# A transformer block in float32: the latent attention's queries and keys turned on VectorE and through DRAM

## The chip, the cores and the metric

The kernel runs on one core of one Trainium2 chip. The metric is the device time of one execution in microseconds (us), lower is better. Of three executions of the kernel before, the median is 890.19 us (889.85 to 890.6).

## The reference, cut to what matters

The program computes a long transformer block for 256 rows of 1024 columns in float32: a gated feed-forward, a mixer of three branches, a second gated feed-forward, and then a second block (a modulated short convolution and a third feed-forward). The mixer holds two attentions. The first is over memory rows. The second is the latent attention with 8 heads, causal, and it is the one that is changed:

```
q = (rmsnorm(c_q, cq_norm) @ w_uq).reshape(B, S, 8, 96)      # S = 256 rows
q = rmsnorm(q, q_norm);  q = concat([q[..., :64], rope(q[..., 64:])])
kv = (rmsnorm(c_kv, ckv_norm) @ w_ukv).reshape(B, S, 8, 128)
k = rmsnorm(concat([k_nope, k_pe]), k_norm);  k = concat([k[..., :64], rope(k[..., 64:])])
s = einsum('bqhd,bkhd->bhqk', q, k) * 96 ** -0.5             # masked, softmax, times v
```

TensorE's matmul sums over partitions. The scores of a head therefore need q and k with the 96 columns of the head on the partitions, while the products leave them with the rows on the partitions: each head's queries and keys must be turned.

The second block is modulated by six rows, `silu(c) @ ada_w + ada_b`, each of 1024 values. The kernel calls c the conditioning.

## The kernel before

**Weights.** All weights stream through one ring of 10 slots in SBUF (`RAW`, tile raw). An entry is a *unit*: two chunks of 128 rows of one product's weights, 128x1024 values, 512 KB. SP's queue fetches entry n+10 once entry n is used up (L1765). ScalarE copies a unit to a rounded high part (`split`, L916), VectorE subtracts it to get the low part (`split`, L1209), and TensorE multiplies high by high, high by low and low by high (L741 to L743), which for one unit and both halves of the rows is 12 matmuls with 512 columns. There are 308 units.

**Order.** `schedule()` writes one list, SCHEDULE, and every engine's queue is the part of that list that it has a function for. `unit(name, i, *steps)` first adds the `split` steps up to four units ahead (AHEAD), then the matmuls, then the side steps. So VectorE and ScalarE have the copies for unit u + 4 in their queues ahead of the side steps of unit u. In the mixer the side steps are given by a table `side`, from the mixer's unit number, 0 to 67, to steps. An engine that waits in one step holds all of its later ones. SP's queue, too, is one list: a fetch stands behind every wait ahead of it.

**Modulation rows.** `stream_of()` mixes 48 further entries of 512 KB into the ring, ("ada", i), each 128 columns of `ada_w`. They are not multiplied on TensorE: VectorE multiplies each by the conditioning row and sums it (L1221). 24 of them run in the first feed-forward (66 units), 24 in the second. The first goes behind unit 10 of the feed-forward, and after that they go at 24 in 50 units:

```
            while ada and i >= 10 and (24 - len(ada)) * 50 < (i - 9) * 24:
                out.append(ada.pop(0))
```

Also in the first feed-forward: at unit 8 SP fetches the memory rows in two forms, 2 MB in all; and the hidden rows are turned without TensorE, in six groups: VectorE turns 32x32 blocks (`blocks`, L1337), SP writes the result to DRAM in four pieces (`spill`, L1820), reads it back in another order (`reload`, L1827), and ScalarE and VectorE make high and low parts of it (`inner`, L998 and L1342). The first group is written at unit 11, reloaded at unit 12 and used by ScalarE at unit 14.

**The latent attention.** Products uq0, uq1, ukv0, ukv1 fill QT and KT, 128 partitions x 2 x 768. `row1` (sums of squares), `row2` (the keys times their norm) and `row3` (rotary part, for q half 0 at unit 30, q half 1 at 32, k half 0 at 33, k half 1 at 34) finish them on VectorE. Then each head goes through five steps that are spread over units by `att`:

```
    def att(k):
        parts = (("att_val", k - 4), ("att_pt", k - 3), ("att_sc", k - 1), ("att_in", k), ("att_exp", k - 1))
        return [p for p in parts if 0 <= p[1] < 8]
    for n in range(12):
        side[37 + 2 * n] = side.get(37 + 2 * n, []) + att(n)
```

`att_in(h)` turns a head: four TensorE transposes into PSUM (L850), then two ScalarE copies with the norm's gain into qkT (L1123, L1124). `att_sc` multiplies scores (L858), VectorE masks them and takes maxima (L1544 to L1549), ScalarE exponentiates (`att_exp`, L1133), TensorE turns the weights (`att_pt`, L865) and multiplies them with V (`att_val`, L874), and VectorE scales the result into U (L1563). TensorE's small results share four PSUM banks in turn (`bank`).

**Around it.** Branch a, the spatial gating: VectorE normalizes V (`sv_norm`, L1485 and L1488; half 0 at unit 32, half 1 at unit 35), TensorE mixes it (`su` at unit 38, L840), VectorE forms two products (L1494, L1500), and TensorE turns the result (`y_turn` "a" at unit 41, L649). Gate additions (L1572, each behind its product's last unit) share VectorE. Branch b, the attention's result, is turned at unit 61 (`y_turn` "b", L649, L1097, L1467), and its product's units are 66 and 67. The conditioning row is loaded for the second time at unit 41, into acc2.

## Time and profile before

| | before |
|---|---|
| median of three executions | 890.19 us |
| the profiled execution | 890.65 us |
| its span, first to last instruction | 888.9 us |
| TensorE (PE) busy | 878.5 us, 99% |
| VectorE (DVE) busy | 631.6 us, 71% |
| ScalarE (ACT) busy | 460.7 us, 52% |
| granted TensorE clock, mean | 0.997 |

The profiled execution took 890.65 us, its span is 888.9 us; the rest lies around the span. Starts of matmuls are recorded, while their ends are modelled, so a busy engine is best read from the distance between starts. A time in the lists is counted from the start of the span. PEld is TensorE's loading of the stationary operand, which overlaps with the matmuls. Lines are those of the kernel before. Where the text counts units, it counts from the start of a feed-forward or, in the mixer, from the mixer's first unit.

### The profile page before, as it was taken

To read this page: it belongs to the slowest core of one execution; us is meant where nothing else is said; L and a number is where in the kernel's file an instruction comes from. 1 tells how busy PE (TensorE), PEld (TensorE's weight loads), DVE (VectorE), ACT (ScalarE), POOL (GpSimd) and SP (SyncE) were. 2 spreads that over 40 slices of the span, in tenths; PEclk is the share of its full clock that TensorE was granted. 3 is DMA by queue.
4 is the path that set the end of the run, shared out by engine and by line. 5 is a ranking of instruction groups with operands and counts; after the bars stand their busy time and mean duration, and the time that the engine had idled before them with its cause. 6 is when DMAs were issued, how large, how long until landed. Compare 5 with 4: busy or idle time off the path is not lost.

```text
span 888.9 us, 11084 instructions
## 1 busy us (share of the span) xinstructions
PE 878.5 (99%) x4079; PEld 732.8 (82%) x4079; DVE 631.6 (71%) x883; ACT 460.7 (52%) x697; POOL 40.8 (5%) x66
## 2 busy tenths in 40 slices
PE   9999999999999999999999999999999999999996
PEld 7878888888998888888888888888888888888885
DVE  6769987837558877688578886875768766665743
ACT  6546554626688475446535554454445344444530
POOL 0010000022103000000000000001000100000000
PEclk9999999999999999999999999999999999999998
DMA  9899999774654454454699999975755577777741
GB/s 365 346 323 352 359 363 351 270 237 145 182 175 175 162 193 164 149 186 143 218 308 348 344 329 323 333 257 163 257 179 177 182 248 241 240 233 246 250 120 47
DMA packets 94879, 215.12 MB, mean 242 GB/s; under 512 B 14520, under 2 KB 46185, under 8 KB 94697
## 3 DMA queue, kind: packets, MB, share of 16 engines
q1 hardware_dynamic: 94104, 212.97, 69.8%
q10 hardware_dynamic: 720, 1.44, 0.4%
q8 instruction: 32, 0.52, 0.2%
q14 instruction: 23, 0.18, 0.1%
HBM read 204.66 MB, written 9.72 MB: 241 GB/s over the span
## 4 chain that ended last, share of the span: by engine, by line
PE 94%; DMA 2%; DVE 1%; issue 1%; ACT 1%; SPq 0%; POOL 0%; POOLq 0%; DVEq 0%
PE ps L741 29%; PE ps L743 29%; PE ps L742 29%; DMA t_raw<-in_f_up 2%; PE ps L679 1%; PE ps L656 1%; PE ps L649 1%; PE ps L858 1%; PE ps L874 1%; PE ps L816 0%; PE ps L850 0%; PE ps L798 0%; DVE t_wl L1209 0%; DMA t_acc<-in_xT 0%; PE ps L865 0%
## 5 line engine op out<-in xcount | busy, mean ns | idle before, releaser
L1209 DVE TENSOR_TENSOR t_wl<-t_raw,t_wh 128x1024 fp32r<-128x1024 f32 (+3 forms) x308 | 360.4, 1203 | 103.3 <-ACT t_wh L916 102.4
L916 ACT ACTIVATE t_wh<-t_raw 128x1024 fp32r<-128x1024 f32 (+3 forms) x308 | 307.8, 1040 | 106.9 <-DMA t_raw<-in_f_up 63.3
L741 PE MATMUL ps<-t_wh,t_XH 128*128 128x512 f32 (+2 forms) x640 | 250.2, 391 | 1.3 <-DVE t_wl L1209 1.3
L743 PE MATMUL ps<-t_wh,t_XL 128*128 128x512 f32 (+2 forms) x640 | 247.1, 386 | 0.0
L742 PE MATMUL ps<-t_wl,t_XH 128*128 128x512 f32 (+2 forms) x640 | 246.8, 386 | 0.0
L741 PEld LDWEIGHTS ps<-t_wh,t_XH 128*128 128x128 f32 x640 | 120.2, 188 | 24.8 <-DVE t_wl L1209 2.1
L743 PEld LDWEIGHTS ps<-t_wh,t_XL 128*128 128x128 f32 x640 | 120.1, 188 | 24.0
L742 PEld LDWEIGHTS ps<-t_wl,t_XH 128*128 128x128 f32 x640 | 120.3, 188 | 22.9
L741 PE MATMUL ps<-t_wh,t_YH 128*128 128x512 f32 x288 | 113.1, 393 | 0.2 <-DVE t_YL L1634 0.2
L743 PE MATMUL ps<-t_wh,t_YL 128*128 128x512 f32 x288 | 112.2, 390 | 0.0
L742 PE MATMUL ps<-t_wl,t_YH 128*128 128x512 f32 x288 | 112.2, 389 | 0.0
L741 PE MATMUL ps<-t_wh,t_HH 128*128 128x512 f32 x264 | 103.0, 390 | 0.0
L743 PE MATMUL ps<-t_wh,t_HL 128*128 128x512 f32 x264 | 102.8, 389 | 0.0
L742 PE MATMUL ps<-t_wl,t_HH 128*128 128x512 f32 x264 | 102.7, 389 | 0.0
L741 PEld LDWEIGHTS ps<-t_wh,t_YH 128*128 128x128 f32 x288 | 54.1, 188 | 11.5 <-issue 0.6
L743 PEld LDWEIGHTS ps<-t_wh,t_YL 128*128 128x128 f32 x288 | 54.1, 188 | 11.2
L742 PEld LDWEIGHTS ps<-t_wl,t_YH 128*128 128x128 f32 x288 | 54.1, 188 | 10.9
L1221 DVE CUSTOM_DVE_ANT_0 t_acc<-t_raw,t_acc 128x1024 f32<-128x1024 f32 x48 | 58.3, 1214 | 6.5 <-issue 3.9
L741 PEld LDWEIGHTS ps<-t_wh,t_HH 128*128 128x128 f32 x264 | 49.6, 188 | 10.4
L743 PEld LDWEIGHTS ps<-t_wh,t_HL 128*128 128x128 f32 x264 | 49.6, 188 | 10.3
L742 PEld LDWEIGHTS ps<-t_wl,t_HH 128*128 128x128 f32 x264 | 49.6, 188 | 10.2
L998 ACT ACTIVATE t_HH<-t_tp 128x512 fp32r<-128x512 f32 (+1 forms) x36 | 19.4, 587 | 40.5 <-DMA t_tp<-inner_rows 40.5
(225 smaller groups left out, 614.1 us busy)
## 6 DMA issues: line engine op xcount, KB each, us to landing
t_raw<-in_f_up SPq DMA_DIRECT2D x130, 512.0 KB, 5.6
t_raw<-in_f_dn SPq DMA_DIRECT2D x66, 512.0 KB, 5.5
t_raw<-in_ada SPq DMA_DIRECT2D x48, 512.0 KB, 6.3
inner_rows<-t_tp SPq DMA_DIRECT2D x60, 128.0 KB, 3.8
t_tp<-inner_rows SPq DMA_DIRECT2D x15, 512.0 KB, 5.2
t_raw<-in_mkv SPq DMA_DIRECT2D x8, 512.0 KB, 3.6
t_raw<-in_ga SPq DMA_DIRECT2D x8, 512.0 KB, 3.3
t_raw<-in_gc SPq DMA_DIRECT2D x8, 512.0 KB, 3.2
```

The source lines that it names most:

```text
L649: m = pe.transpose(o, src[:, t, (c + i) * P:(c + i) * P + P], ident[:, :])
L656: m = pe.transpose(ps[:, b, c * P:c * P + P], src[:, t, (4 * j + c) * P:(4 * j + c) * P + P], ident[:, :])
L679: x = pe.matmul(ps[:, bank_of("f1_up0", t), :], a[:, k, t * P:t * P + P], w, start=a is XH and not last and k == 0, stop=last and k == KC - 1)
L741: pe.matmul(o, xh, h, start=k == 0, stop=False)
L742: pe.matmul(o, xh, l, start=False, stop=False)
L743: x = pe.matmul(o, xl, h, start=False, stop=k == n - 1)
L858: m = pe.matmul(ps[:, b, t * P:t * P + n], qkT[0:96, t * P:t * P + P], qkT[0:96, 256:256 + n], start=True, stop=True)
L874: m = pe.matmul(ps[:, b, t * 64:t * 64 + 64], pT[:, j * P:j * P + P], VT[:, kt, h * 64:h * 64 + 64], start=kt == 0, stop=kt == t)
L916: act.activation(wh[:, m % SPL, lo:w], raw[:, n % RAW, lo:w], ACT.Copy).then_inc(hi_made, 1)
L998: act.activation(parts_of(HH, q, t), placed(q, t), ACT.Copy).then_inc(*hid_hi.by(f, q, t))
L1209: dve.tensor_tensor(wl[:, n % RAW, lo:w], raw[:, n % RAW, lo:w], wh[:, m % SPL, lo:w].bitcast(F32), ALU.subtract).then_inc(drained, 1)
L1221: dve.tensor_tensor_reduce(out=acc2[:, 1, :], in0=r, in1=cond, scale=1.0, scalar=0.0, op0=ALU.mult, op1=ALU.add, accum_out=mod[:, i:i + 1] ...
```

## The change

Four things are changed.

1. `att_in` has no part on TensorE any more. VectorE turns 32x32 blocks of all heads' queries (`qk_blocks` "q" at mixer unit 33) and keys (at unit 35), two instructions of 128x768 for each. SP writes them to DRAM in four pieces each (`qk_out`, units 34 and 36) and reads them back with the head's columns on 96 partitions (`qk_back`, units 35 and 37). ScalarE's two copies into qkT now read SBUF; the first head's wait for both reloads.
2. The attention's steps start at unit 39 instead of 37, and branch b is turned at unit 63 instead of 61.
3. The 24 modulation rows of the first feed-forward start behind unit 18 instead of 10 and go at 24 in 42 units.
4. The queries come back into acc2, where the conditioning row went; this is loaded at unit 57 instead of 41, behind the eighth head's copies. The keys come back into a new tile KB, which lies over QT and a part of KT.

```diff
+        start = 18 if tag == "f1" else 10
         for i, u in enumerate(part):
             out.append(u)
-            while ada and i >= 10 and (24 - len(ada)) * 50 < (i - 9) * 24:
+            while ada and i >= start and (24 - len(ada)) * (60 - start) < (i - start + 1) * 24:
                 out.append(ada.pop(0))
...
-            35: [("sv_norm", 1)], 38: [("su", 0), ("su", 1)], 41: [("y_turn", "a", 0), ("y_turn", "a", 1), ("load_cond", 1)],
-            61: [("y_turn", "b", 0), ("y_turn", "b", 1)]}
+            35: [("sv_norm", 1)], 38: [("su", 0), ("su", 1)], 41: [("y_turn", "a", 0), ("y_turn", "a", 1)],
+            57: [("load_cond", 1)], 63: [("y_turn", "b", 0), ("y_turn", "b", 1)]}
...
+    for n, x, step in ((33, "q", "qk_blocks"), (34, "q", "qk_out"), (35, "q", "qk_back"),
+                       (35, "k", "qk_blocks"), (36, "k", "qk_out"), (37, "k", "qk_back")):
+        side[n] = side.get(n, []) + [(step, x)]
     for n in range(12):
-        side[37 + 2 * n] = side.get(37 + 2 * n, []) + att(n)
+        side[39 + 2 * n] = side.get(39 + 2 * n, []) + att(n)
...
+        qk_mid = {"q": hn[:, :, :].rearrange("p t d -> p (t d)")[:, 0:1536], "k": QT[:, :, :].rearrange("p t d -> p (t d)")}
+        qk_end = {"q": acc2[:, :, :].rearrange("p t d -> p (t d)"), "k": KB[:, :]}
...
-            def att_in(h):
-                b = bank(("att_in", h), qkt_made, h + 1)
-                if h == 0:
-                    pe.wait_ge(*qk_made.at("k", 1))
-                for i, src in enumerate((QT, KT)):
-                    for t in (0, 1):
-                        m = pe.transpose(ps[0:96, b, i * 256 + t * P:i * 256 + t * P + P], src[:, t, h * 96:h * 96 + 96], ident[:, :])
-                m.then_inc(turned, 1)
...
             def att_in(h):
-                b, full = place["att_in", h]
-                act.wait_ge(turned, full)
                 if h:
                     act.wait_ge(turned, place["att_sc", h - 1][1])
-                act.activation(qkT[0:96, 0:256], ps[0:96, b, 0:256], ACT.Copy, scale=qkg[0:96, 0:1])
-                act.activation(qkT[0:96, 256:512], ps[0:96, b, 256:512], ACT.Copy, scale=qkg[0:96, 1:2]).then_inc(qkt_made, 1)
+                else:
+                    act.wait_ge(qk_in["q"], 16)
+                    act.wait_ge(qk_in["k"], 16)
+                for n, x in enumerate("qk"):
+                    m = act.activation(qkT[0:96, 256 * n:256 * n + 256].rearrange("p (t i n) -> p t i n", t=2, i=4),
+                                       qk_end[x][0:96].rearrange("p (i t h n) -> p h t i n", i=4, t=2, h=8)[:, h],
+                                       ACT.Copy, scale=qkg[0:96, n:n + 1])
+                m.then_inc(qkt_made, 1)
...
+            def qk_blocks(x):
+                dve.wait_ge(*qk_made.at(x, 1))
+                for t in (0, 1):
+                    m = dve.transpose(qk_mid[x][:, 768 * t:768 * t + 768].rearrange("p (j h n) -> p h j n", j=3, h=8),
+                                      (QT if x == "q" else KT)[:, t, :].rearrange("p (h j n) -> p h j n", j=3, h=8))
+                m.then_inc(qk_blocked[x], 1)
...
             def load_cond(n):
                 if n:
-                    sp.wait_ge(*qk_mean.at("k", 1))
+                    sp.wait_ge(qkt_made, 8)
...
+            def qk_out(x):
+                sp.wait_ge(qk_blocked[x], 1)
+                for i in range(4):
+                    sp.dma_start(qk_rows["qk".index(x), i].rearrange("b f e -> f b e"),
+                                 qk_mid[x][32 * i:32 * i + 32, :].rearrange("f (b e) -> f b e", b=6)).then_inc(qk_out_done[x], 16)
+            def qk_back(x):
+                sp.wait_ge(qk_out_done[x], 64)
+                sp.dma_start(qk_end[x][0:96].rearrange("p (b e) -> p b e", b=8),
+                             qk_rows["qk".index(x)].rearrange("i (t j) f e -> (j f) (i t) e", t=2)).then_inc(qk_in[x], 16)
```

## Rows read from the trace of the kernel before

**Rows 1.** The page: busy time by engine, share of span, instructions.
```profile
PE 878.5 (99%) x4079; PEld 732.8 (82%) x4079; DVE 631.6 (71%) x883; ACT 460.7 (52%) x697; POOL 40.8 (5%) x66
```

**Rows 2.** TensorE's timeline: start, duration, line, operation; idle before and releaser.
```profile
57.55 0.39 PE L743 MATMUL ps<-t_wh,t_XL 128*128 128x512 f32 x1
59.08 0.50 PE L741 MATMUL ps<-t_wh,t_XH 128*128 128x512 f32 x1 [1.15 <-DVE t_wl L1209]
...
61.71 0.39 PE L743 MATMUL ps<-t_wh,t_XL 128*128 128x512 f32 x1
62.25 0.50 PE L741 MATMUL ps<-t_wh,t_XH 128*128 128x512 f32 x1 [0.16 <-DVE t_wl L1209]
```

**Rows 3.** Chain of waits, 25 to 70 us: start, duration, what.
```profile
50.32 6.36 DMA t_raw<-in_f_up
```

**Rows 4.** ScalarE's timeline, 45 to 60 us.
```profile
53.80 1.15 ACT L998 ACTIVATE t_HH<-t_tp 128x512 fp32r<-128x512 f32 x2 [4.43 <-DMA t_tp<-inner_rows]
...
56.70 1.06 ACT L916 ACTIVATE t_wh<-t_raw 128x1024 fp32r<-128x1024 f32 x1 [0.72 <-DMA t_raw<-in_f_up]
```

**Rows 5.** Two stretches: length, busy time by engine, clock, DMA share, GB/s.
```profile
62.00:110.00 48.00, 47.84 (x211) 39.53 (x211) 46.89 (x84) 28.40 (x45) 0.00 (x0) 1.00 0.97 347
290.00:310.00 20.00, 19.98 (x107) 16.80 (x106) 16.07 (x26) 7.97 (x14) 0.00 (x0) 1.00 0.46 158
```

**Rows 6.** Chain of waits, 293.5 to 304 us.
```profile
294.23 0.61 PE ps L850 x4
...
302.78 0.44 PE ps L850 x4
```

**Rows 7.** TensorE's timeline around the turning of the second head.
```profile
301.96 0.82 PE L858 MATMUL ps<-t_qkT 96*128 96x128 f32 x4
...
303.29 0.39 PE L742 MATMUL ps<-t_wl,t_XH 128*128 128x512 f32 x1
```

**Rows 8.** TensorE's timeline around the last scores.
```profile
353.89 0.82 PE L858 MATMUL ps<-t_qkT 96*128 96x128 f32 x4
...
354.78 0.40 PE L742 MATMUL ps<-t_wl,t_XH 128*128 128x512 f32 x1
```

**Rows 9.** Line 1337: duration in ns, minimum, median, maximum; forms.
```profile
L1337 DVE STREAM_TRANSPOSE t_tp<-t_hp x18: 711/1245/1248, 34.4 to 826.3; 128x1024 f32<-128x1024 f32 x15, 128x512 f32<-128x512 f32 x3
```

**Rows 10.** VectorE's timeline, 289 to 306 us.
```profile
290.61 1.22 DVE L1209 TENSOR_TENSOR t_wl<-t_raw,t_wh 128x1024 fp32r<-128x1024 f32 x1
...
295.92 0.69 DVE L1488 TENSOR_TENSOR t_V<-t_V,t_gates 128x512 f32<-128x512 f32 x1
...
298.80 1.28 DVE L1572 TENSOR_TENSOR t_gates<-ps,t_bgate 128x512 f32<-128x512 f32 x2
...
304.91 0.69 DVE L1500 TENSOR_TENSOR t_U<-t_U,t_V 128x512 f32<-128x512 f32 x1
```

**Rows 11.** TensorE's timeline around the spatial matmuls.
```profile
297.44 1.95 PE L840 MATMUL ps<-t_V,t_sgw 128*128 128x128 f32 x16
299.14 0.48 PE L741 MATMUL ps<-t_wh,t_XH 128*128 128x512 f32 x1
```

**Rows 12.** Timeline of all engines and SP's queue, 122 to 131 us.
```profile
122.33 2.01 SPq L1820 DMA_DIRECT2D inner_rows<-t_tp  x4
...
126.30 0.38 SPq L1827 DMA_DIRECT2D t_tp<-inner_rows  x1
...
130.75 0.63 ACT L998 ACTIVATE t_HH<-t_tp 128x512 fp32r<-128x512 f32 x1 [4.92 <-DMA t_tp<-inner_rows]
```

**Rows 13.** Timeline of all engines, 379 to 382 us.
```profile
379.04 1.03 PE L649 MATMUL ps<-t_ident,t_U 128*128 128x128 f32 x8
...
380.30 1.29 DVE L1467 TENSOR_TENSOR t_YL<-ps,t_YH 128x512 fp32r<-128x512 f32 x2 [3.87 <-ACT t_YH L1097]
```

**Rows 14.** Timeline of all engines, 147 to 149.5 us.
```profile
147.14 1.23 DVE L1209 TENSOR_TENSOR t_wl<-t_raw,t_wh 128x1024 fp32r<-128x1024 f32 x1 [4.24 <-ACT t_wh L916]
...
149.45 0.39 PE L741 MATMUL ps<-t_wh,t_HH 128*128 128x512 f32 x1
```

More of the change, by code:

```diff
@@ L423, in build @@
             MV = sb("MV", [P, 2, 512], F32, c)
-            QT = sb("QT", [P, 2, 768], F32, c)
-            KT = sb("KT", [P, 2, 768], F32, c)
+            with ExitStack() as c2:
+                QT = sb("QT", [P, 2, 768], F32, c2)
+                KT = sb("KT", [P, 2, 768], F32, c2)
+            KB = sb("KB", [P, 2048], F32, c)
+            sb("qk_rest", [P, 1024], F32, c)
             VT = sb("VT", [P, 2, 512], F32, c)
@@ L484, in build @@
         drop = nc.dram_tensor("mod_rows", (48, P), F32, kind="Internal").ap()
+        qk_rows = nc.dram_tensor("qk_rows", (2, 4, 6, 32, 256), F32, kind="Internal").ap()
         inner_rows = nc.dram_tensor("inner_rows", (4, 8, 32, P), F32, kind="Internal").ap()
@@ L551, in build @@
         k_rope = sem("k_rope")
+        qk_blocked, qk_out_done, qk_in = ({x: sem(f"qk_{n}_{x}") for x in "qk"} for n in ("blocked", "out", "in"))
         v_cent, v_sq, v_mean, v_rstd, v_made = (sem("v_" + n) for n in ("cent", "sq", "mean", "rstd", "made"))
@@ L899, in _ @@
                     "mem_in": mem_in_, "mem_sc": mem_sc, "mem_pt": mem_pt, "mem_val": mem_val, "y_turn": y_turn,
-                    "su": su, "att_in": att_in, "att_sc": att_sc, "att_pt": att_pt, "att_val": att_val,
+                    "su": su, "att_sc": att_sc, "att_pt": att_pt, "att_val": att_val,
                     "mturn": mturn, "conv_turn": conv_turn, "gate_turn": gate_turn}
@@ L1654, in _ @@
                     "sv_mean": sv_mean, "sv_sq": sv_sq, "sv_norm": sv_norm, "su": su, "row1": row1, "row2": row2, "row3": row3,
-                    "att_sc": att_sc, "att_pt": att_pt, "att_val": att_val, "gate": gate, "merge": merge,
+                    "qk_blocks": qk_blocks, "att_sc": att_sc, "att_pt": att_pt, "att_val": att_val, "gate": gate, "merge": merge,
                     "mturn": mturn, "conv_uu": conv_uu, "conv_taps": conv_taps, "gate_turn": gate_turn, "gate_low": gate_low,
@@ L1872, in _ @@
                     "load_cond": load_cond, "ada_rows": ada_rows, "load_mod": load_mod,
-                    "load_mid": load_mid, "gate": gate, "load_final": load_final, "final": final, "spill": spill, "reload": reload}
+                    "load_mid": load_mid, "gate": gate, "load_final": load_final, "final": final, "spill": spill, "reload": reload, "qk_out": qk_out, "qk_back": qk_back}
             for name, *args in SCHEDULE:
```

## The prediction

> **What bounds the kernel now.** I read the page first: TensorE is busy for 878.5 us, 99% of the span [rows 1]. In such a kernel only two things shorten the run: matmul instructions taken off TensorE, and waits of TensorE. So the next view is TensorE's own timeline, looking for starts further apart than usual. The twelve matmuls of one weight unit start at 59.08 (first) to 61.71 (last): 0.1 us extra behind the first, then 0.23 each, 2.72 us a unit. Between the entry and the attention there are two wide gaps: 57.55 to 59.08 and 61.71 to 62.25, both ended by VectorE's low part of a weight unit; less the usual 0.23 they cost 1.3 and 0.3 us, 1.6 in all [rows 2]. The chain of waits says what lies under it: a weight transfer asked for at 50.3 us that landed 6.4 us later [rows 3]. ScalarE's timeline says what stood in its queue ahead of the unit concerned, number 19: the high part of the reloaded hidden rows (start 53.80), a square of the memory rows, and then the unit's own copy at 56.70, which waited 0.72 us for the transfer; ScalarE was free from 56.0 [rows 4]. From there to 110 us the DMA engines are 97% busy and VectorE 46.9 of 48 us [rows 5]: this stretch is near two other limits. In the attention TensorE's timeline has no such gap; there the price of an edit is what TensorE itself executes, plus any wait that is made new.
>
> **Part 1: the turning leaves TensorE.** Removed are 8 heads of 4 transposes. In the chain one head's four take 0.44 us, and the first head's takes 0.61 since they came behind a wait [rows 6]. The timeline agrees: with them [rows 7], from the first score matmul to the second weight matmul it is 301.96 to 303.29 = 1.33 us; after the last head, where none follow, 353.89 to 354.78 = 0.89 [rows 8]. So 7 x 0.44 + 0.6 = **3.7 us off TensorE**. Nothing hides this term, as TensorE is the bound.
>
> The Trainium skill speaks against this edit: VectorE: DVE Perf Modes, section "Rules for kernel authors", gives a 128x128 transpose to TensorE when PSUM may be its destination, as VectorE turns only 32x32 blocks. By that rule the path without TensorE would cost more than 3.7 us; by the rows so far it costs less, and rival C is the case in which the rule has it.
>
> **Part 2: what comes in on VectorE.** Four block transposes of 128x768. The trace has 128x1024 at 1.24 and 128x512 at 0.71 us [rows 9], hence 0.98 each alone, and some 0.1 less back to back, as its neighbours overlap: 1.8 us per pair (1.6 to 2.4, if the scattered output costs as much as a 128x1024 one). The queries' pair goes in right behind the first rotary step of the keys, before the subtraction at 290.61; VectorE has no gap from there to 299. So everything after is 1.8 us later on VectorE, up to the second V normalization, whose addition starts at 295.92 and ends at 296.61 [rows 10]. That one matters: TensorE's spatial matmuls wait for it and now start at 297.44 [rows 11], 0.83 us after it. New: it ends at 298.4, while TensorE arrives at 296.8, as the first head's 0.6 us ahead of it is gone. **A new wait of 1.6 us.** (The low part for the unit between, 1.1 us long, is ready at 293.6 and wanted at about 294.0, so it just holds.)
>
> The keys' pair goes in behind that addition. VectorE: 298.4 + 1.8 = 300.2, then two weight subtractions (2.3), so the gate additions start at 302.5 in place of 298.80. From their start to the end of the second product for branch a it is now 304.91 + 0.69 - 298.80 = 6.8 us [rows 10], new end 309.3. TensorE: spatial matmuls 298.45 to 300.15 (1.70 as now, [rows 11]), three units of 12 matmuls (2.72 each and 0.1 for the first), so it reaches the turning of branch a at 308.4, the second half at 308.85, and waits for the second product until 309.35: **0.5 us**. It is done with it at 309.8 and wants the first scores.
>
> **Part 3: the way through DRAM.** The keys' route ends last. The nearest row is the hidden rows' route of the same form: blocks ended at 122.3, the four writes issued from 122.33, the reload issued at 126.30, ScalarE's first use at 130.75: 8.4 us [rows 12]. Here each way has 786 KB in place of 512, but 1 KB pieces in place of 512 B and DMA engines that are 46% busy from 290 to 310 us rather than 97% [rows 5]. I take 9 us: 300.2 + 9.0 = 309.2, and ScalarE's two copies (0.9) give 310.1 against TensorE's 309.8: **0.3 us**. Bounds: 7.5 us for the route would hide it (slack 1.2); 13 us (each of the two ways 2.3 us longer than its row) costs 4.3. Queued behind this wait: on ScalarE, which blocks at it from about 306, the copies of mixer units 44 and 45, wanted by TensorE only at about 317 and 320 (scores 0.7 us, two units, scores), while their copies and subtractions can be done 3 to 5 us behind the first head's: at least 3 us of cover more than the scores have; on SP's queue, which blocks first for the queries' blocks (about 286 to 292), then for each write, the fetches of four weight units, each some 6 to 9 us late, with ten slots in the ring and about 18 us until they are wanted. Both are hidden as long as the first scores are the ones that wait.
>
> **Other edits of the middle.** The step order of the heads is kept, two matmul units later each; ScalarE's copies read the same 256 elements from SBUF, and their PSUM banks now turn over between three users. Later by two units is the turning of branch b. Its low part comes 1.3 + 1.3 us after TensorE's start (379.04, end 381.6, [rows 13]); it now has two units, 5.4 us, instead of four before the product that wants it. Late next would be the first product of branch b, from a delay of about 2.5 us. The conditioning row, fetched 16 units later, is wanted more than ten units after that. All three: nothing.
>
> **Part 4: the modulation rows of the first feed-forward.** The 24 of them start after unit 18 instead of 10 and are denser (one in 1.75 units instead of 2.08). The ring holds ten entries, and an entry is a weight unit or such a row. Without the rows, ten entries are ten units: unit 19 is asked for when unit 10 is done (unit 11 starts eight units ahead of 57.8, the undelayed start of unit 19: 57.8 - 8 x 2.72 = 36 us) and not behind the reload at 50.3, so its landing no longer counts. ScalarE's queue still has the reload in front: if that lands as now, unit 19's copy starts at 56.0 rather than 56.70 and 0.7 us are gained; if two fewer 512 KB transfers ahead of the write bring it 1 to 2 us sooner, the wait is gone, and the small one at 62.25 with it. Bounds 0.7 and 1.6; I take **1.2 us gained**. From unit 24 to 60 the look-ahead is six units where it was six or seven, and the entries per unit grow from 1.48 to 1.57, or 6%, in a stretch that is 97% busy. A narrow place late in it is unit 52: low part ended 148.4, wanted 149.45 [rows 14], 1.1 us of cover. I cost this at nothing, as the rows' total up to there is the same to within one; without the cover each 1 us is 1 us.
>
> **Sum.** -3.7 + 1.6 + 0.5 + 0.3 - 1.2 = -2.5. The profiled execution took 890.65 us (span 888.9 and 1.8 around it), 0.46 above the median of 890.19. So 888.15 for it, and **887.7 as median**.
>
> **Rivals.** For orientation: +-0.2% is 1.8 us, about what a measurement of this kernel can tell from no change.
> A. The waits are covered: VectorE's pairs cost less at their place, the route takes under 8 us, and the early wait goes whole. -3.7 - 1.6 = -5.3, median 884.9. Against it: VectorE has no gap before 298.8, so at least 1.4 of the 1.6 should show. Partly so (one wait smaller) is inside the forecast's own range.
> B. The early wait stays, because it hangs on the 2 MB of memory rows and on the reload in ScalarE's queue and not on the modulation rows: -3.7 + 2.4 = -1.3, median 888.9, no change that can be told. For it: the reload alone holds unit 19 until 56.0.
> C. Slower: the route through DRAM. ScalarE stops at the first head until the keys are back, and TensorE at its scores. Each microsecond beyond 9 is one lost; it decides (above +1.8) from 13.3 us for the route. With 14.5 us: -2.5 + 5.5 = +3.0, median 893.2. For it: two transfers in a row that each carry half as much again, and a queue that issues them one behind the other. Against it: 8.4 us for the smaller route with the DMA engines twice as busy.
> D. The denser modulation rows empty the ring towards unit 52 and again at 85 to 110 us, where VectorE is nearly full: one or two waits of 1 to 2 us, together 2.5: median 890.2, the same.
>
> **How the numbers follow.** Forecast 0.45, A 0.15, B 0.20, C 0.11, D 0.09. The forecast's own range is 886.6 (route hidden, early gain 1.6, pairs of 1.6 us) to 889.7 (route 10.5 us, early gain 0.7). For 8 in 10 over all cases: from A's 884.9 to 891.0, which holds B and D and leaves out most of C and D's bad end. Faster by over 0.2% (below 888.4): three quarters of the forecast (0.34), A, and a quarter of B (0.05): 0.54. Slower (above 892.0): C's greater part and a little of D: 0.11. The same: 0.35.
>
> **What would show it.** No PE wait at 57 to 62 us, or a smaller one (part 4). Four block transposes of about 0.9 us near 290.6 and 298.4. PE waiting about 1.6 us at the spatial matmuls for V, and 0.5 at branch a's turning for U. The reload of the keys at about 304 and its landing at 308 to 309; ScalarE's qkT copy ended by that landing. Wrong would be the forecast if VectorE had slack ahead of V, if PE waited over 3 us at the first scores, or if PE waits showed up between 70 and 160 us.

## The result and the profile after

The changed kernel takes 902.44 us (median of 4 executions, 902.02 to 904.82) against 890.33 us for the kernel before (4 executions). The ratio is 1.0142 with a 95% interval of 1.0124 to 1.016: slower by some 12 us, where 2.5 us faster was predicted. Its profiled execution took 902.61 us, span 900.9.

The page answers to [rows 1] in busy time by engine. Each engine does what it did, TensorE 32 instructions less; the 12 us are waits.

```profile
PE 878.8 (98%) x4047; PEld 729.9 (81%) x4047; DVE 634.7 (70%) x887; ACT 459.9 (51%) x697; POOL 43.2 (5%) x66
```

TensorE's waits by line and releaser: us in total, times, longest.

```profile
PE ps L865 <- ACT t_qkT L1132: 5.6, 1, 5.6
PE ps L757 <- DVE t_wl L1220: 5.0, 6, 1.8
...
PE ps L856 <- issue: 1.5, 1, 1.5
PE ps L695 <- ACT t_wh L958: 0.8, 2, 0.6
```

L757 is the weight matmul (L741 before), L865 the scores, L856 the spatial matmuls. L695 belongs to the first product; its waits lie before 17 us, where the two kernels are still 0.05 us apart. I then subtracted the starts of the same weight unit's matmuls in the two traces. This offset is -0.44 us at unit 20 of the first feed-forward (62 us), 1.64 at unit 33, 2.93 at unit 40, 5.78 at unit 48 (145 us), and stays there until the attention. It falls to 5.2 (the first head's transposes are gone), rises to 6.9 at the spatial matmuls and to 13.4 behind the first scores, falls by 0.44 per further head to 10.3, and ends at 11.9, as the heads' last steps, two units later than before, are then made up. So there are two losses of about 6 us each, 150 us apart.

**The first feed-forward.** The stretch of [rows 5], columns as there. TensorE's busy time is 1.3 us short of the 48, but it started 201 matmuls instead of 211, and the offset grew by 2.7 us from 62 to 110 us. The DMA engines were busy less (0.86 instead of 0.97) and VectorE too (44.33 us instead of 46.89): none of the three was busy throughout.

```profile
62.00:110.00 48.00, 46.69 (x201) 37.10 (x201) 44.33 (x80) 23.68 (x36) 0.00 (x0) 1.00 0.86 314
```

The chain from 40 to 62 us begins at SP's issue of the hidden rows' writes (L1839), goes through their landing and the reload's, and comes to VectorE's blocks of the next group (L1348), which are what SP waits for again:

```profile
43.26 5.84 DMA inner_rows<-t_tp
49.12 3.89 DMA t_tp<-inner_rows
...
58.25 1.26 DVE t_tp L1348
59.53 0.33 SPq L1839
```

In the timeline of the same stretch the reload had landed at 53.0, 0.8 us sooner than before. ScalarE stood 10.72 us for it (4.43 before, [rows 4]) because it had made the copies ahead of it sooner, not because it came late. VectorE multiplied two modulation rows (L1232) before the low part at 60.54:

```profile
53.03 1.16 ACT L1005 ACTIVATE t_HH<-t_tp 128x512 fp32r<-128x512 f32 x2 [10.72 <-DMA t_tp<-inner_rows]
...
54.91 1.22 DVE L1232 CUSTOM_DVE_ANT_0 t_acc<-t_raw,t_acc 128x1024 f32<-128x1024 f32 x1
...
59.42 1.18 DVE L1232 CUSTOM_DVE_ANT_0 t_acc<-t_raw,t_acc 128x1024 f32<-128x1024 f32 x1
...
60.54 1.22 DVE L1220 TENSOR_TENSOR t_wl<-t_raw,t_wh 128x1024 fp32r<-128x1024 f32 x1
```

The low part at 60.54 is what TensorE waited 1.3 us for at unit 20. It stood behind the blocks (58.25) and the row at 59.42 on VectorE; in the kernel before, one row ran at 55.67 and the next only at 62.12, behind that low part. The wait at unit 19 [rows 2] is gone.

**The attention.** The timeline of all engines around the way of the keys:

```profile
296.45 1.83 DVE L1552 STREAM_TRANSPOSE t_hn<-t_QT 128x768 f32<-128x768 f32 x2
...
302.35 0.39 PE L759 MATMUL ps<-t_wh,t_XL 128*128 128x512 f32 x1
...
303.14 0.30 SPq L1856 DMA_DIRECT2D t_acc<-qk_rows  x1
303.49 0.69 DVE L1499 TENSOR_TENSOR t_V<-t_V,t_gates 128x512 f32<-128x512 f32 x1
...
304.10 1.83 DVE L1552 STREAM_TRANSPOSE t_QT<-t_KT 128x768 f32<-128x768 f32 x2
...
304.28 2.02 PE L856 MATMUL ps<-t_V,t_sgw 128*128 128x128 f32 x16 [1.54 <-issue]
...
305.95 3.03 SPq L1851 DMA_DIRECT2D qk_rows<-t_QT  x4
...
314.48 0.30 SPq L1856 DMA_DIRECT2D t_KB<-qk_rows  x1
...
320.19 0.51 ACT L1132 ACTIVATE t_qkT<-t_acc,t_sc 96x256 f32<-96x256 f32 x1 [8.26 <-DMA t_KB<-qk_rows]
```

Both pairs of blocks took 1.83 us. TensorE's spatial matmuls came 1.93 us after the matmul ahead of them, 1.70 more than the usual 0.23. The keys' route took from 305.9 (blocks ended) to 320.19: 14.3 us, of which 8.5 passed until all four writes had landed and the reload could be issued, and 5.7 for the reload. TensorE's timeline of the first scores and of what follows:

```profile
321.24 1.20 PE L865 MATMUL ps<-t_qkT 96*128 96x128 f32 x3 [5.57 <-ACT t_qkT L1132]
...
322.31 0.99 PE L757 MATMUL ps<-t_wh,t_XH 128*128 128x512 f32 x1
323.09 0.63 PE L758 MATMUL ps<-t_wl,t_XH 128*128 128x512 f32 x1
323.52 0.63 PE L759 MATMUL ps<-t_wh,t_XL 128*128 128x512 f32 x1
...
325.23 0.48 PE L757 MATMUL ps<-t_wh,t_XH 128*128 128x512 f32 x1
325.54 0.40 PE L758 MATMUL ps<-t_wl,t_XH 128*128 128x512 f32 x1
```

Behind the wait of 5.6 us the weight matmuls start 0.43 us apart instead of 0.23, until 325.2. The windows give a granted clock of 0.83 from 310 to 330 us, where the stretches around have 1.00: for some 4 us TensorE ran at the lower of its two levels, 1.2 GHz. From the first score matmul to the second weight matmul it is 1.85 us where it was 0.89 [rows 8], and from there to 325.54 it is 2.45 where six distances of 0.227 make 1.36. The slower starts cost 2.05 us on top of the wait.

```profile
310.00:330.00 20.00, 14.33 (x61) 11.59 (x59) 10.96 (x16) 10.78 (x20) 0.00 (x0) 0.83 0.66 226
```

### The profile page after: what moved, and what is told of

Same layout as the page of the kernel before. It is cut to its first block, busy times and chain, and to the rows that moved or that the text cites. A ratio compares the mean times of both kernels' runs of the same rounds, so it can differ in the third digit from the quotient of the medians.

```text
span 900.9 us, 11027 instructions
## 1 busy us (share of the span) xinstructions
PE 878.8 (98%) x4047; PEld 729.9 (81%) x4047; DVE 634.7 (70%) x887; ACT 459.9 (51%) x697; POOL 43.2 (5%) x66
## 4 chain that ended last, share of the span: by engine, by line
PE 79%; DVE 8%; DMA 7%; ACT 2%; issue 2%; SPq 1%; POOL 0%; POOLq 0%; ACTq 0%; DVEq 0%
PE ps L757 25%; PE ps L759 25%; PE ps L758 25%; DVE t_wl L1220 3%; DMA t_raw<-in_f_up 2%; DMA inner_rows<-t_tp 1%; DMA t_tp<-inner_rows 1%; PE ps L672 1%; PE ps L695 1%; DVE t_acc L1232 1%; SPq L1839 1%; ACT t_wh L923 1%; PE ps L865 1%; DMA qk_rows<-t_QT 1%; DMA t_hn<-in_xT 1%
## 5 line engine op out<-in xcount | busy, mean ns | idle before, releaser
L757 PE MATMUL ps<-t_wh,t_XH 128*128 128x512 f32 (+2 forms) x640 | 251.8, 393 | 3.3 <-DVE t_wl L1220 3.2
L757 PEld LDWEIGHTS ps<-t_wh,t_XH 128*128 128x128 f32 x640 | 120.6, 188 | 29.3 <-DVE t_wl L1220 6.5
L757 PE MATMUL ps<-t_wh,t_YH 128*128 128x512 f32 x288 | 113.4, 394 | 0.2 <-DVE t_YL L1653 0.2
L757 PE MATMUL ps<-t_wh,t_HH 128*128 128x512 f32 x264 | 103.1, 391 | 1.8 <-DVE t_wl L1220 1.8
L757 PEld LDWEIGHTS ps<-t_wh,t_YH 128*128 128x128 f32 x288 | 54.1, 188 | 11.6 <-issue 0.6
L758 PEld LDWEIGHTS ps<-t_wl,t_YH 128*128 128x128 f32 x288 | 54.1, 188 | 10.9
L757 PEld LDWEIGHTS ps<-t_wh,t_HH 128*128 128x128 f32 x264 | 49.6, 188 | 12.6 <-DVE t_wl L1220 2.2
L1232 DVE CUSTOM_DVE_ANT_0 t_acc<-t_raw,t_acc 128x1024 f32<-128x1024 f32 x48 | 58.3, 1214 | 0.0
L1353 DVE TENSOR_TENSOR t_HL<-t_tp,t_HH 128x512 fp32r<-128x512 f32 (+1 forms) x36 | 21.6, 643 | 29.6 <-ACT t_HH L1005 29.6
```

The lines of the kernel that those rows point to most:

```text
L757: pe.matmul(o, xh, h, start=k == 0, stop=False)
L758: pe.matmul(o, xh, l, start=False, stop=False)
L1232: dve.tensor_tensor_reduce(out=acc2[:, 1, :], in0=r, in1=cond, scale=1.0, scalar=0.0, op0=ALU.mult, op1=ALU.add, accum_out=mod[:, i:i + 1] ...
L1353: dve.tensor_tensor(parts_of(HL, q, t), placed(q, t), parts_of(HH, q, t).bitcast(F32), ALU.subtract).then_inc(*hid_lo.by(f, q, t))
```

## The experiments

Each ratio is to the kernel before, run on the same chip. "Alone" means the kernel before with that one edit.

### Which part costs what

The modulation rows alone (`r1_rows18`, its edit is shown), and the changed kernel with the old rows (`r2_way10`, which sets `start = 10` in the changed kernel).

```diff
-            while ada and i >= 10 and (24 - len(ada)) * 50 < (i - 9) * 24:
+            start, end = (18, 60) if tag == "f1" else (10, 60)
+            while ada and i >= start and (24 - len(ada)) * (end - start) < (i - start + 1) * 24:
```

> The kernel before with part 3 of the change alone (modulation rows of the first feed-forward behind unit 18 instead of 10, 24 in 42 units). If the two halves of the change add up, this one gives the 5.8 us by which the mixer starts later in the changed kernel: about 896. Rival: the way through DRAM's queue steps and the rows interact (both load SP's queue), then this alone is under 893.

> The changed kernel with the modulation rows back at unit 10, 24 in 50 units. If the halves add up: 902.4 - 5.8 = about 896.5, with the 5.6 us wait at the first scores as in the changed kernel. Rival: in the changed kernel the wait was long because of what the first feed-forward had displaced; then it is under 3 us here and the time under 893.

Measured: rows alone 896.95 us, 1.0063 (1.0041 to 1.0084); the route with the old rows 896.5 us, 1.0062 (1.004 to 1.0084). The two add up to 1.0125, the whole is 1.0142 (1.0124 to 1.016): within the intervals they are the whole. In the first, TensorE's waits for low parts are 5.1 us in 6, as in the changed kernel; in the second, 6.1 us at the first scores and 1.5 for V. Each half of the change is slower by itself, and for its own reason. In the profiled execution of `r1_rows18` 1.7 us of the loss is the clock: behind a wait of 1.81 us at unit 48 the weight matmuls start 0.43 us apart from 144.8 to 147.8, and the granted clock from 110 to 160 us is 0.97. The changed kernel had a wait of 1.76 us at the same unit and kept a clock of 1.00.

### The rows: later, or denser

The same line with (10, 52), 24 rows in 42 units but from unit 10, and with (18, 65), from unit 18 but in 47 units.

> The kernel before with the rows as dense as in the change (24 in 42 units) but from unit 10 on, so they end at unit 52. Theory look-ahead: ten ring entries are only six units wherever rows are dense, and the loop of VectorE's blocks, SP's waits, fetch and ScalarE's copy cannot be run through in six units; so this loses 4 to 6 us as well, about 895. Rival position: what hurts is that the rows' products are moved into units 24 to 60, behind the memory rows' parts and the rotary tables on VectorE; then this is within 1.5 us of before.

> The kernel before with the rows behind unit 18 but nearly as sparse as before (24 in 47 units, one in 1.96), up to unit 65. Theory look-ahead: part of the units keep seven units of look-ahead, so the loss falls well below that of the dense order: 0 to 2.5 us, 890 to 892.5. Rival position: the loss stays at 4 us or more.

Measured: from unit 10 and dense 898.65 us, 1.0078 (1.0051 to 1.0106); from unit 18 and less dense 891.69 us, 1.0004 (0.9993 to 1.0015). (In the first, 1.7 us more of TensorE's waits are for the turning of the rows themselves.) So the later start by itself shows no cost and no gain; the density costs the 5 to 6 us, although it is a change from one row in 1.96 units (47) to one in 1.75 (42).

### What a row loads

With the rows of `r1_rows18`: each of the 24 rows fetched at half its bytes (`m1_half_bytes`; the multiplication reads the half twice), or fetched whole and multiplied in half its columns (`m2_half_vector`). The modulation that comes out is not the reference's in either. And the kernel before with `RAW = 9`, one slot less in the ring (`m6_ring9`). Of the first edit the line with the width is shown.

```diff
-    return 1024 if name == "ada" else W_OF[name] * min(2, K_OF[name] - 2 * i)
+    return (512 if i < 24 else 1024) if name == "ada" else W_OF[name] * min(2, K_OF[name] - 2 * i)
```

```diff
+                h = 512 if i < 24 else 1024
+                dve.tensor_tensor_reduce(out=acc2[:, 1, 0:h], in0=r[:, 0:h], in1=cond[:, 0:h], scale=1.0, scalar=0.0, op0=ALU.mult, op1=ALU.add,
```

```diff
-RAW = 10
+RAW = 9
```

> The kernel before with the later and denser rows (r1, +6 us), but each of the 24 row entries transfers only 512 of its 1024 columns, and VectorE multiplies those twice, so its time is kept; the second half of each sum is left out. Theory DMA traffic: with 256 KB less per entry the transfers land in time and the 6 us are gone, about 891. Theory VectorE in the loop: the ring slots and VectorE's queue are what they were, so over 3 us stay, about 894 or more.

> The same rows order (r1, +6 us) with full transfers, but VectorE multiplies and sums only the first 512 columns of each of the 24 entries (0.5 us less each; the rest of the sum is left out). Theory VectorE in the loop: its queue is what delays the block transposes, behind which SP's queue stands, so most of the 6 us are gone, about 891. Theory DMA traffic: no change against r1, about 896.

> The kernel before, rows as before, with 9 ring slots instead of 10. Theory look-ahead: nine entries are about six units at 1.48 entries a unit, what the denser order left of ten, without any more bytes or VectorE work per unit; so this costs about as much as r1 in the first feed-forward (+4 to +8 us) and something in the second as well. Theory throughput: the work per unit is that of before, so under +2 us.

Measured: 893.64 us, 1.0031 (1.0016 to 1.0047) with half the bytes; 893.56 us, 1.0017 (1.0008 to 1.0026) with half the multiplication; 900.07 us, 1.0094 (1.0079 to 1.0109) with nine slots. Halving the bytes brought the DMA share of 62 to 110 us down to 0.79; halving the multiplication brought VectorE to 41.3 of 48 us. The two medians are 2.3 us above the kernel before, the intervals overlap, and TensorE's waits for low parts are 3.5 us in both traces: each leaves a quarter to a half of the loss, and which of the two leaves less isn't resolved. Neither transfer rate nor VectorE's time is the bound by itself. Look-ahead matters with the rows left as they were: with one slot of ten gone, the kernel before loses 8.4 us. In the profiled execution the offset grows by 8.7 us in the first feed-forward, a dip of the clock at unit 48 included, and by 1.7 us more at 709 us. A row takes a slot, and thereby look-ahead from the weight units.

### The loop through SP's queue

With the rows of `r1_rows18`, the writes and reloads of the hidden rows' groups issued by GpSimd's queue (`m3_pool_spill`), or by SP one unit later than now (`m4_spill_later`, groups 1 to 3, whose edit comes first). Of the other edit a part is shown; it moves the writes and reloads of all three feed-forwards.

```diff
-            ways = (3, 4, 6) if (f, q) == ("f1", 0) else (0, 1, 3 if q == 4 else 4)
+            ways = (3, 4, 6) if (f, q) == ("f1", 0) else (1, 2, 3 if q == 4 else 4) if f == "f1" and q < 4 else (0, 1, 3 if q == 4 else 4)
```

```diff
             def spill(f, q):
-                sp.wait_ge(*blocked.at(f, q))
+                pool.wait_ge(*blocked.at(f, q))
...
```

> r1 (the kernel before with the later, denser rows, +6 us) with all writes and reloads of the hidden rows issued from GpSimd's queue, where nothing waits behind them, instead of SP's. Theory loop: the waits come from SP's queue standing at the blocks' write (26 us in 60 to 165 us) while weight fetches wait behind; unblocked, the fetches go out when their slot is free and TensorE's waits at 70 to 150 us vanish, also the one at 60; 890 or less. Theory throughput (DMA engines and VectorE simply near full): at least half of the 6 us stay. GpSimd's queue may have a cost per transfer of its own, which would show in the reload's landing.

> r1 (later and denser rows, +6 to +7 us) with the write and reload of the first feed-forward's hidden groups 1 to 3 one unit later in the queues (group 0 was later already, 4 and 5 stay), their use unchanged. Theory loop through SP's stand: SP waits about 2.7 us less per group at VectorE's blocks while a fetch goes out in between, so TensorE's waits fall by 2 to 5 us. Rival: the stand is only where the lateness shows, and a later reload makes ScalarE wait; then the time stays or grows.

Measured: on GpSimd's queue 930.78 us, 1.0421 (1.0367 to 1.0476), with waits of 30.4 us for low parts, 18.2 of them in the first feed-forward and 12.2 behind 500 us. From 60 to 165 us a write there took 4.7 us to land and a reload 6.5 (2.2 and 5.1 from SP's queue in `r1_rows18`). It tells of that queue's price, not of the loop, and part of that price lies outside the stretch in question. One unit later on SP's queue: 891.88 us, 1.0009 (1.0 to 1.0018). It gives back 5 of the 6 us. The waits of `r1_rows18` (first SP's queue for the blocks in VectorE, then TensorE):

```profile
SPq L1821 <- DVE t_tp L1338: 41.0, 9, 7.2
```

```profile
PE ps L742 <- DVE t_wl L1210: 5.1, 6, 1.8
```

and of `m4_spill_later`:

```profile
SPq L1821 <- DVE t_tp L1338: 25.9, 9, 5.8
```

```profile
PE ps L742 <- DVE t_wl L1210: 1.6, 3, 1.1
```

SP stands for 15 us less, and TensorE's waits for low parts are 1.6 us, near the 1.3 of the kernel before. My reading of it, argued from these traces: rows 1.75 units apart and SP's stand at the blocks feed each other: VectorE is late, so SP issues late, so the fetches behind are late, so ScalarE's copies and VectorE's low parts are, and VectorE reaches the next blocks later.

### The transposes by themselves

The kernel before without the 32 transposes (`c1_no_turning`): ScalarE copies 96 partitions of the unturned rows, so that the scores are of other numbers.

```diff
-            def att_in(h):
...
-                        m = pe.transpose(ps[0:96, b, i * 256 + t * P:i * 256 + t * P + P], src[:, t, h * 96:h * 96 + 96], ident[:, :])
-                m.then_inc(turned, 1)
```

> The kernel before without the queries' and keys' turning: TensorE's 32 transposes are left out and ScalarE copies the same number of elements straight from QT and KT, so scores are of wrong values. It measures the term by itself: -3.7 us, about 887.0 beside a before of 890.9. Rival: other waits take its place at once and under 2 us are gained.

Measured: 887.34 us against 891.42, 0.9955 (0.9942 to 0.9967): 4.0 us. That is all that taking the turning off TensorE can give back here.

### The way through DRAM

All start from `r2_way10` (old rows). `n1_no_q_route` leaves the queries' writes and reload out (acc2 holds other numbers); `n5_reload_alone` is that, and SP waits for the keys' reload before it issues the fetches behind it; `x1_pool_route` issues both routes from GpSimd's queue; `n3_two_later` moves the attention two units on, its last steps to units 58, 59 and 61.

```diff
-    for n, x, step in ((33, "q", "qk_blocks"), (34, "q", "qk_out"), (35, "q", "qk_back"),
+    for n, x, step in ((33, "q", "qk_blocks"),
...
-                    act.wait_ge(qk_in["q"], 16)
```

```diff
+                sp.wait_ge(qk_in[x], 16)
```

```diff
             def qk_out(x):
-                sp.wait_ge(qk_blocked[x], 1)
+                pool.wait_ge(qk_blocked[x], 1)
...
```

```diff
-        side[39 + 2 * n] = side.get(39 + 2 * n, []) + att(n)
+        u = {9: 58, 10: 59, 11: 61}.get(n, 41 + 2 * n)
+        side[u] = side.get(u, []) + att(n)
```

> r2 (changed kernel with the rows at unit 10, 896.5) without the queries' writes and reload: ScalarE copies what lies in acc2, so the queries are wrong values, and only the keys go through DRAM. The keys' route took 14.3 us from the end of its blocks to ScalarE, where 9 were forecast. Theory collision: the queries' reload (8.2 us in flight) holds the keys' writes up; alone the keys' route takes 9 to 10 us, the wait at the first scores is under 1.5 us, no dip of the clock, about 890.5. Theory own size: the keys' route stays at 13 us or more, and so does the wait; about 896.

> n1 (no queries' route, 896.3) and SP's queue also waits for the keys' reload to land before it issues the fetches it has held back. In n1 the writes went through in 4.8 us, but the reload took 8.7, with four weight fetches issued within 3.5 us behind it. Theory shared engines: alone the reload lands in 4 to 5.5 us, the route is 10 us from the blocks' end, the wait at the first scores falls from 4.8 to about 1.5 us and the low clock behind it goes: about 891.5. Theory form (96 partitions, 1 KB pieces): the reload stays near 8 us and the time near 896.

> r2 (896.5) with the four steps of the way through DRAM on GpSimd's queue instead of SP's, so that weight fetches are not held back behind its waits and do not come in a burst behind the reload. Theory shared engines: the keys' reload meets at most one fetch, and the route falls from 14.8 us to about 12; the wait at the first scores from 6 to about 3: 893.5. Rival: GpSimd's queue issues so much slower that the route is as long or longer, 896 or more.

> r2 with every step of the attention two units later again (first head at unit 41) and the last three steps closer together, so that branch b's turning stays at unit 63. The 5.6 us wait at the first scores has 5.4 us more cover and should be gone, and with it the low clock behind it (about 1.7 us): 896.5 - 5.5 - 1.7 = about 889.3, if nothing new waits. Rival: ScalarE still stands at the first head and now holds later units' copies, or the closer last steps make waits of their own; then over 892.

In the table the keys' writes are counted from the end of their blocks to the issue of their reload, and the reload from there to ScalarE's first copy.

| | ratio (95%) | us | keys: writes, reload | wait at the first scores |
|---|---|---|---|---|
| `r2_way10` | 1.0062 (1.004 to 1.0084) | 896.5 | 8.9, 5.9 | 6.1 |
| `n1_no_q_route` | 1.0053 (1.0038 to 1.0068) | 896.33 | 4.8, 8.7 | 4.8 |
| `n5_reload_alone` | 1.0034 (1.0021 to 1.0047) | 894.65 | 4.8, 6.3 | 2.5 |
| `x1_pool_route` | 1.0098 (1.0081 to 1.0115) | 900.5 | 10.9, 6.4 | 8.6 |
| `n3_two_later` | 0.999 (0.998 to 0.9999) | 890.35 | 8.5, 6.2 | 0.6 |

Without the queries' transfers the keys' writes land in 4.8 us instead of 8.9: the difference is the queries' way, whose reload is under way at the same time (8.4 us in `r2_way10`), with the weight fetch that SP held back for it. But little is won, as the reload then takes 8.7 us, with four fetches issued within 3.5 us behind it; with these kept off it takes 6.3. With both kept off the route takes 11.1 us instead of 14.8, a quarter less. The fetches behind it can't be the whole reason for 8.7: in `r2_way10` and in the changed kernel four fetches followed the reload just as closely, and it took 5.9 and 5.7. That stays open. On GpSimd's queue the keys' writes begin only at 302.2, 1.9 us behind the end of their blocks, as the queue stands until the queries' writes have landed, and each write takes 6.3 us to land (4.7 in `r2_way10`): the route takes 17.3 us. Two units (about 6 us) more time hide the route nearly whole:

```profile
PE ps L857 <- issue: 1.5, 1, 1.5
PE ps L866 <- ACT t_qkT L1133: 0.6, 1, 0.6
PE ps L758 <- DVE t_wl L1221: 0.6, 1, 0.6
```

Its interval only just excludes 1, and it is one of eighteen ratios; `b1_way_and_spill` below differs from it by the later writes alone and comes to 0.9997. So it is as fast as the kernel before, and that it is faster isn't shown. Of the 4.0 us V's wait takes 1.5 and the first scores 0.6. The 0.6 us for the low part lie in the first feed-forward, where the kernel before waits 1.3 us in its own trace. The rest isn't traced.

### V's norm, and all three waits at once

`n2_blocks_behind_norm` (from `r2_way10`) and `n4_both` (from `n3_two_later`) do both pairs of blocks at unit 35, behind V's norm. `b1_way_and_spill` is `n3_two_later` with the writes of `m4_spill_later`. `b2_norm_34` moves V's second norm to unit 34 ahead of the keys' blocks, has the attention's steps from unit 42 (the first scores at 44), and the later writes too. Of the edit of the first two a line is left out by which the keys' blocks wait for the queries'; then that of the last, without the writes:

```diff
-    for n, x, step in ((33, "q", "qk_blocks"), (34, "q", "qk_out"), (35, "q", "qk_back"),
-                       (35, "k", "qk_blocks"), (36, "k", "qk_out"), (37, "k", "qk_back")):
+    for n, x, step in ((35, "q", "qk_blocks"), (35, "k", "qk_blocks"), (36, "q", "qk_out"), (36, "k", "qk_out"),
+                       (37, "q", "qk_back"), (37, "k", "qk_back")):
...
```

```diff
-            32: [("row3", "q", 1), ("sv_norm", 0)], 33: [("row2", 0), ("row3", "k", 0)], 34: [("row2", 1), ("row3", "k", 1)],
-            35: [("sv_norm", 1)], 38: [("su", 0), ("su", 1)], 41: [("y_turn", "a", 0), ("y_turn", "a", 1)],
+            32: [("row3", "q", 1), ("sv_norm", 0)], 33: [("row2", 0), ("row3", "k", 0)], 34: [("row2", 1), ("row3", "k", 1), ("sv_norm", 1)],
+            38: [("su", 0), ("su", 1)], 41: [("y_turn", "a", 0), ("y_turn", "a", 1)],
...
-        side[39 + 2 * n] = side.get(39 + 2 * n, []) + att(n)
+        u = {8: 58, 9: 59, 10: 60, 11: 61}.get(n, 42 + 2 * n)
+        side[u] = side.get(u, []) + att(n)
```

> r2 (896.5) with both pairs of block transposes behind V's second norm, all writes at unit 36 and both reloads at 37. The wait of 1.5 us ahead of the spatial matmuls goes. The keys' blocks end when they did, but now the queries' writes are still ahead of the keys': the wait at the first scores grows from 6 to about 8. Together about 896.5. Rival: the spatial matmuls wait as before, since the norm itself is late for another reason.

> n3 (attention two units later again, 890.35) with the blocks behind the norm as in n2. If the spatial matmuls' wait was the queries' blocks: 1.5 us less, about 888.9, minus up to 2 if the keys are back only after the first scores want them (n3 had 0.6 us of wait there). This is the version to which the runs point: turning off TensorE -3.7, all covers kept.

> The version with the attention two units later and rows of 18 from unit 10 came to 0.999, with waits of 1.5 us for V's norm, 0.6 at the first scores and 0.6 for the low parts. Here the writes and the reloads of the first feed-forward's groups are issued one unit later besides. If the loop through SP's stand at the blocks is what still costs there, SP's stand falls below 16 us and the waits of the first feed-forward fall by 0.5 to 1.5 us: ratio 0.9970 to 0.9985. If the density of the rows itself is the cost, nothing changes: 0.999.

> V's norm is moved ahead of both pairs of block transposes, the first scores come at unit 42, and the groups' writes and reloads of the first feed-forward one unit later. If the price of the change is made of three waits (V's norm 1.5 us, the route at the first scores 5.6, the fetch loop 5), and each is a matter of place, all three go and what is left is the 4.0 us of TensorE's transposes less some 0.4 to 1: ratio 0.9955 to 0.9970. If the route keeps its price wherever it stands, a wait of 2 us or more is left at the first scores: ratio above 0.998.

Measured: 900.28 us, 1.0096 (1.0083 to 1.011) for `n2_blocks_behind_norm`; 892.57 us, 1.0018 (1.0009 to 1.0027) for `n4_both`; 890.24 us, 0.9997 (0.9988 to 1.0005) for `b1_way_and_spill`; 894.81 us, 1.0049 (1.0036 to 1.0063) for `b2_norm_34`. With the blocks behind the norm V's wait is gone; branch a's turning waits 1.5 and 1.6 us instead, and the first scores 7.2 and 1.4. The later writes gave nothing to the kernel with the old rows, so what they cure is the dense rows. In `b2_norm_34` the wait for V is 0.4 us and none is left at the first scores, as expected; new ones have come elsewhere. Of TensorE's waits these are the ones to compare (L666 is branch a's turning; those for low parts, L1221, lie in the first feed-forward, where the kernel before has 1.3 us):

```profile
PE ps L882 <- ACT t_pT L1153: 2.2, 1, 2.2
...
PE ps L758 <- DVE t_hn L1603: 1.5, 1, 1.5
PE ps L758 <- DVE t_wl L1221: 1.1, 3, 0.5
PE ps L666 <- DVE t_U L1512: 1.0, 2, 0.7
```

My reading is that on even units an attention step shares its place with the gates and the merges at the end of a product; that was not tried apart. ScalarE's timeline shows the longest: the copy of the turned weights that TensorE wants stands behind two gates and a weight unit's copy,

```profile
370.49 1.23 ACT L1159 ACTIVATE t_gates<-t_gates 128x512 f32<-128x512 f32 x2 [1.89 <-DVE t_gates L1592]
371.62 1.04 ACT L924 ACTIVATE t_wh<-t_raw 128x1024 fp32r<-128x1024 f32 x1
372.57 0.47 ACT L1153 ACTIVATE t_pT<-ps 128x384 f32<-128x384 f32 x1
```

and behind that wait the weight matmuls again start 0.43 us apart, from 375.5 to 376.8. My expectation named three waits and took every other step's place as free, which it wasn't.

## Why the prediction was wrong

**The step that failed: "I cost this at nothing"** (part 4, the density of the rows). The argument was that "the rows' total up to there is the same to within one", with a look-ahead of six units where it was six or seven. What the runs showed is that the stretch has next to no reserve of look-ahead: 24 rows in 47 units cost nothing that can be told, the same rows in 42 units 5 to 6 us, and one slot of ten 8.4. In the changed kernel it came to 6.2 us between units 20 and 48. The signs were there, the DMA engines at 97% and VectorE at 46.9 of 48 us [rows 5], and were taken for two limits near by. SP's queue, which holds its fetches while it waits for the blocks, is the link between them that the prediction didn't price: its writes issued one unit later gave 5 of the 6 us back. Rival D named the stretch and less than half of the price (2.5 us).

**Mis-sized: "I take 9 us"** (part 3, the route). It took 14.3 us, so that the wait at the first scores was 5.6 us instead of 0.3; the step from one to the other was right (14.3 - 9.0 = 5.3). The 9 us came from one route by itself [rows 12], and its share of bandwidth from a stretch in which the new transfers were not yet there. Here the keys' writes ran beside the queries' reload: 8.5 us to the issue of the reload instead of 4.0; the run without the queries' way has 4.8. The reload itself took 5.7 instead of 4.4. Rival C had this, with 14.5 us as its example, but at 0.11; and behind it the sum lacked a term of 2.05 us, the slower clock that was found behind that wait.

**C and D as exclusive cases.** They have no cause in common, and both came; together they gave a time far above the range, which held D by itself and left out most of C.

**Too hopeful: 1.2 us gained early.** The wait of unit 19 went (offset -1.36 there), as part 4 had it. At unit 20 TensorE waited 1.3 us instead: the prediction didn't ask what would be late next once unit 19 was not. What is left at unit 20 is a gain of 0.5 us (from 0.05 to -0.44). `r4_rows18_65`, which has the late start without the density, shows nothing gained (1.0004). Rival B's price for this term is near, but by luck: in B the wait of unit 19 stays, and it went in every trace with the late start. Besides, the 1.3 us were one execution's: in the ten other traces with the old rows and ten slots, unit 19 comes between 0.65 us sooner and 0.4 us later against the units ahead of it than in the trace that was read.

**Right: the turning off TensorE**, 3.7 us predicted, 4.0 measured by `c1_no_turning`. **Right: the blocks**, 1.8 us a pair predicted and 1.83 in the trace. **Right: the wait for V**, 1.6 predicted, 1.7 by the starts. As for the rule of the Trainium skill that part 1 weighed (VectorE: DVE Perf Modes, section "Rules for kernel authors"), the trace agrees with its outcome for this order of steps: the path without TensorE cost more than 3.7 us. VectorE's share of that was 2.0 us (V's wait 1.7, branch a's turning 0.3); the larger part was the way through DRAM, 5.6 us of wait and 2.05 of slower clock. With the attention two units later (`n3_two_later`) the path cost about what it saved. **Nearly: branch a's turning**, 0.5 predicted, 0.3 found. **Right: the later turning of branch b and the conditioning row**: no wait of TensorE there.

The sum with the measured terms: -4.0 + 1.7 + 0.3 + 5.6 + 2.05, with -0.5 (up to unit 20) and +6.2 (from there to unit 48), makes +11.35 for the profiled execution, against 902.61 - 890.65 = 12.0. The 0.6 us between them aren't accounted for; 0.25 of them may lie in the first term, as the offset of `c1_no_turning` falls by 3.75 us over the attention.

**Open.** How the 6 us of the dense rows divide between transfers and VectorE isn't settled: the two halvings gave back, by the medians, 3.8 of 6.1 us each, more than the whole together, so that they are no shares of a sum. That the rows, SP's stand and the late low parts form a loop is the reading that fits them all; only one of its links, SP's order, was cut by itself. That the granted clock fell because of the wait is what several traces show beside each other, and wasn't tried apart. Whether a table exists that has all three waits hidden and no new one isn't known; `b2_norm_34` was one attempt.

## What to carry to other kernels

When a queue fetches through a ring and also waits for computed data, price a denser ring by its look-ahead and not by the totals: take one slot away, and see what it costs. Price a route through DRAM with the transfers that run beside it, those of the change itself above all, and count what its queue held back and issues behind it. Two rivals with separate causes can both come: give them a case together.

## What was not expected of the hardware

- After TensorE had stood for 5.6 us its matmuls started 0.43 us apart for some 3 us (granted clock 0.83 in the stretch), and after 2.2 us in `b2_norm_34` for 1.3 us: a wait cost up to 2 us more than itself. After 1.81 us in `r1_rows18` it cost 1.7 us more, after 1.76 us at the same unit in the changed kernel nothing.
- The same reload of 786 KB took 5.7 us in the changed kernel, 5.9 in `r2_way10`, 6.3 in `n5_reload_alone`, 8.7 in `n1_no_q_route` and 9.9 in `n2_blocks_behind_norm`, where the queries' reload was issued 2.1 us ahead of it.
- Writes and reloads on GpSimd's queue took 4.7 to 6.3 and 6.2 to 6.5 us; in `m3_pool_spill`, over all three feed-forwards, TensorE's waits for low parts were 30.4 us instead of 5.1.
